# A 32-column product ahead of every second up-projection chunk

## The chip, the cores and the metric

The kernel runs on one core of a Trainium2 chip. The metric is the device time of one execution in microseconds (us). Three runs of the kernel before gave 2378.91, 2389.10 and 2390.35 us; their median is 2389.1 us. A further execution was profiled, and all rows below are of that one.

## The reference

Two transformer stacks of two layers run one after the other on 256 tokens with a model width of 1024, in float32. The first one (convolution, neighbourhood and window attention) is not touched by the change. The second one has, in each of its two layers, a feed-forward part, a mix of three attentions, and a feed-forward part again:

```python
def _swiglu(x, w1, w2):
    gt, up = jnp.split(x @ w1, 2, axis=-1)
    return (jax.nn.silu(gt) * up) @ w2
...
for l in range(DEPTH):                                    # DEPTH = 2
    x = _layer_norm(DN_ALPHA * x + 0.5 * _swiglu(x, ffn1_w1[l], ffn1_w2[l]), ...)
    mix = _token_mix(x, ...)
    x = _layer_norm(DN_ALPHA * x + mix, ...)
    x = _layer_norm(DN_ALPHA * x + 0.5 * _swiglu(x, ffn2_w1[l], ffn2_w2[l]), ...)
```

The hidden width is 2816, so `w1` is 1024 x 5632 and `w2` is 2816 x 1024. There are four such feed-forward parts.

## The kernel before

**Layout.** Activations lie transposed in SBUF, with the features on the 128 partitions and the 256 tokens along the free axis: `x[:, k, 0:256]`, `k` from 0 to 7. Weights come from one long stream in DRAM in chunks of 128 x 2048 floats (16 tiles of 128 x 128, 1 MB). A ring of four buffers in SBUF receives them; SyncE issues the DMAs (L210).

**Three products for one.** Each float32 operand is split into a high and a low part of the type `fp32r`: ScalarE rounds a chunk from `ring` to `w_hi` (L226), VectorE subtracts and writes `w_lo` (L240), both in two halves. `w_hi` and `w_lo` have two buffers each, for the even and the odd chunk. `three` (L280 to 284) then multiplies `w_hi` by the high part of the activations, `w_hi` by the low part, and `w_lo` by the high part, into one place of PSUM. Each call of `pe.matmul` becomes a weight load (PEld, 128 x 128) and a product (PE, 256 columns).

**A feed-forward stage** (`ffn_stage`) has 22 up-projection chunks and 11 down-projection chunks, and there are four stages: `ffn_stage` is called twice in each of two layers. An up-projection chunk holds the 8 tiles of the gate and the 8 tiles of the up half for 128 hidden units, so it takes 16 x 3 = 48 products; `pe_columns` writes the gate part to the first 256 columns of its place in PSUM and the up part to the next 256. ScalarE applies SiLU to the gate part (`gate`, L1895), VectorE multiplies (`hid`, L1915), GpSimd splits the result into `h_hi` and `h_lo` (L1946, L1948). A down-projection chunk takes 48 products too (L1871 to L1874, the last chunk through L282 to L284), into eight places of PSUM that stay there over the whole stage.

**Order.** Chunks come in pairs (i, s): `i` counts pairs, and s = 0 or 1 is the chunk in the pair. The first pair (the first two in the first stage) is written out, the others are the body of a hardware loop, with the same instructions and SBUF and PSUM addresses in every turn. In a stage that follows a layer norm the first chunk goes through `pe_side_by_side`. PSUM places alternate with the chunk. TensorE waits in `pe_acc` until the place was read, and in `pe_half` until a half of the chunk was split; both come ahead of the first product of the chunk, `pe_half` again ahead of the ninth tile.

**Where else short products stand in the trace.** In the attention of the second stack, products of 16 columns (L767) and transposes of 128 columns (L796) stand between the full products of L282 to L284. The prediction uses those.

Of the kernel before, what the change touches and what calls it, by code (L numbers as in the profile page):

```python
# [26 lines left out]
P = 128  # L27
D = 1024
KT = D // P
S = 256  # L30
# [85 lines left out]
def build(nc, wstream, xT, ctxT, cT, consts, vecs, rpb, rel, out):  # L116
    ctx = ExitStack()
    with ctx:
        names = {}

        def sb(name, shape, dt=F32, stack=ctx, side="left"):
            names[name] = names.get(name, 0) + 1
            if names[name] > 1:
                name = f"{name}_{names[name]}"
            return stack.enter_context(nc.sbuf_tensor(name, shape, dt, side=side))

        def count(name):
            return Count(ctx.enter_context(nc.semaphore(name)))
# [3 lines left out]
        w_hi = sb("w_hi", [P, 2, CB * P], F32R)  # L132
# [50 lines left out]
        half_read = count("half_read")  # L183
# [81 lines left out]
        def acc(s, n, at=0):  # L265

            a = 2048 * ((g0[0] + s) % 2) + at
            return psum[:, a:a + n]

        def pe_half(pe, i, s, half):  # L270

            pe.wait_ge(split_done.sem, 2 * (g0[0] + s) + 1 + half + 4 * i)

        def pe_acc(pe, i, s):

            c = g0[0] + s
            if c > 1 or not isinstance(i, int) or i:
                pe.wait_ge(acc_free.sem, c - 1 + 2 * i)

        def three(pe, o, w_cols, c, hi, lo, first, last):  # L280

            pe.matmul(o, w_hi[:, c, w_cols], hi, start=first, stop=False)  # L282
            pe.matmul(o, w_hi[:, c, w_cols], lo, start=False, stop=False)  # L283
            return pe.matmul(o, w_lo[:, c, w_cols], hi, start=False, stop=last)  # L284

        def pe_columns(pe, i, s, hi, lo, tok, kt=KT, before=None, out=None, half_read=None):

            if out is None:
                pe_acc(pe, i, s)
                out = acc(s, CB // kt * tok)  # L290
            c = (g0[0] + s) % 2
            for m in range(CB // kt):
                for k in range(kt):
                    n = m * kt + k
                    if n % (CB // 2) == 0:
                        pe_half(pe, i, s, 2 * n // CB)
                    if before and m == 0:
                        before(k)
                    mm = three(pe, out[:, m * tok:m * tok + tok], slice(n * P, n * P + P), c, hi(k), lo(k), k == 0,
                               k == kt - 1)  # L300
                    if half_read and n == CB // 2 - 1:
                        mm.then_inc(half_read.sem, 1)
            mm.then_inc(chunk_done.sem, 1)

        def pe_side_by_side(pe, hi, lo, before, tok=S):

            pe_acc(pe, 0, 0)
            pe_half(pe, 0, 0, 1)
            for k in range(KT):
                before(k)  # L310
                for m in range(2):
                    mm = three(pe, acc(0, tok, m * 512), slice((m * KT + k) * P, (m * KT + k + 1) * P), g0[0] % 2,
                               hi(k), lo(k), k == 0, k == KT - 1)
            mm.then_inc(chunk_done.sem, 1)
# [43 lines left out]
        def keep_awake(pe, n, at):  # L358

            for _ in range(n):
                pe.matmul(psum[:, at:at + P], const("ident"), const("ones_model"), start=True, stop=True)
# [1431 lines left out]
        def ffn_stage(layer, norm, more=True, bias=None):  # L1795
# [10 lines left out]
            with ExitStack() as st:  # L1806
# [5 lines left out]
                def first(i, s):  # L1812
                    return isinstance(i, int) and (i, s) == (0, 0)

                def pairs_of(eng, chunk, between=None):

                    for i in range(lead):
                        chunk(i, 0)
                        chunk(i, 1)
                        if between:  # L1820
                            between(eng, i)
                    with eng.Fori(lead, up // 2) as i:
                        chunk(i, 0)
                        chunk(i, 1)

                with nc.Block() as block:
                    @block.sync
                    def _(sp):
                        if bias:
                            bias.sync(sp)  # L1830
                        each_chunk(sp, min(up + down, CHUNKS - RING - g0[0]), lambda i, s: load_one(sp, i, s))

                    @block.tensor
                    def _(pe):
                        hi, lo = (lambda k: x_hi[:, k, at:at + S]), (lambda k: x_lo[:, k, at:at + S])
                        if norm:
                            keep_awake(pe, 6, 1536)

                        def up_chunk(i, s):
                            if norm and first(i, s):  # L1840
                                pe_side_by_side(pe, hi, lo, lambda k: norm.before(pe, k))
                            else:
                                pe_columns(pe, i, s, hi, lo, S)
                        pairs_of(pe, up_chunk, bias and bias.pe)

                        def last_chunk(i, s):

                            c = (g0[0] + s) % 2
                            pe_half(pe, up // 2 + i, s, 1)
                            pe.wait_ge(lower.sem, l0 + 2 * s + 2 + 4 * i)  # L1850
                            for m in order:
                                o = psum[:, 512 * m:512 * m + S]
                                for k in range(2):
                                    kt = 4 * i + 2 * s + k
                                    b = (k * KT + m) * P
                                    mm = three(pe, o, slice(b, b + P), c, h_hi[:, kt, :], h_lo[:, kt, :], False, k == 1)
                                mm.then_inc((chunk_done if m == order[-1] else tile_done).sem, 1)

                        def chunk(i, s, start):

                            c = (g0[0] + s) % 2
                            for k in range(2):
                                pe_half(pe, up // 2 + i, s, k)
                                kt = 4 * i + 2 * s + k
                                pe.wait_ge(lower.sem, l0 + 2 * s + k + 1 + 4 * i)
                                for m in order:
                                    if start and k == 0 and m == order[-2]:
                                        pe.wait_ge(acc_free.sem, g0[0] + up)
                                    b = (k * KT + m) * P
                                    o = psum[:, 512 * m:512 * m + S]  # L1870
                                    pe.matmul(o, w_hi[:, c, b:b + P], h_hi[:, kt, :], start=start and k == 0,  # L1871
                                              stop=False)
                                    pe.matmul(o, w_hi[:, c, b:b + P], h_lo[:, kt, :], start=False, stop=False)  # L1873
                                    mm = pe.matmul(o, w_lo[:, c, b:b + P], h_hi[:, kt, :], start=False, stop=False)  # L1874
                            mm.then_inc(chunk_done.sem, 1)
                        pe.wait_ge(acc_free.sem, g0[0] + up - 1)
                        chunk(0, 0, True)
                        chunk(0, 1, False)
                        with pe.Fori(1, down // 2) as i:
                            chunk(i, 0, False)  # L1880
                            chunk(i, 1, False)
                        last_chunk(down // 2, 0)
                        moments.pe(pe, (acc_free.sem, g0[0] + up + down))
# [1145 lines left out]
```

## Time and profile before

| | |
|---|---|
| median of three runs | 2389.1 us (2378.91 to 2390.35) |
| profiled execution, its own time | 2399.49 us |
| its span, first to last instruction | 2397.7 us |
| mean granted TensorE clock | 0.995 |
| TensorE busy, products / weight loads | 2310.4 / 2080.9 us |
| VectorE / ScalarE / GpSimd busy | 1498.1 / 1190.8 / 244.1 us |
| up-projection of stage 1, 2, 3, 4: first to last `gate` | 1025 to 1151, 1524 to 1641, 1721 to 1838, 2211 to 2323 us |

A product is shown on PE with its start and a modelled length, which is longer than the distance to the next start, since products are pipelined; the pace of the stream is the distance between starts, or the number of products in a window. Matmuls of other tiles can stand between two rows of one line. The windows view counts an instruction in each window that it touches.

### The profile page before, as it was taken

The page shows a single profiled execution, that of the slowest core. Times are in us where ns is not written, and L with a number is a line of the kernel's source. Part 1 is how long each engine was busy: PE and PEld are TensorE (multiplying, and loading weights), DVE is VectorE, ACT ScalarE, POOL GpSimd, SP SyncE. Part 2 cuts the span into 40 slices and gives each one's busy share as a digit, 9 for nine tenths or more (in the row PEclk, how much of TensorE's full clock was granted, in tenths as well). Part 3 has the DMA queues.
Part 4 walks back from the last instruction along what each step waited for, and adds up shares of the span by engine and source line. Part 5 has one row for each costly group of instructions (what it writes and reads, how often), then busy time and mean ns, then how long its engine had stood idle before and what let it go on. Part 6 is the DMA issues. An engine that isn't in the chain of part 4 may idle for free. (4 is left out here: it accounts for less than half of the span.)

```text
span 2397.7 us, 45036 instructions
## 1 busy us (share of the span) xinstructions
PE 2310.4 (96%) x17296; PEld 2080.9 (87%) x17296; DVE 1498.1 (62%) x2663; ACT 1190.8 (50%) x1934; POOL 244.1 (10%) x272
## 2 busy tenths in 40 slices
PE   6999999999989999999999899999999998999998
PEld 4777677778878689999988899999999988999998
DVE  5487874453568875655476766655655578567654
ACT  6244743543345556434366555533534466555443
POOL 0012000000012000023010100121122001000320
PEclk9999999999999999999999999999999999999999
DMA  7321023444233035455554335455455454344552
GB/s 288 120 75 58 2 106 141 160 156 158 88 121 115 19 137 180 176 197 189 192 168 156 134 133 193 153 182 193 151 182 193 149 199 136 135 165 147 205 193 88
DMA packets 61844, 355.61 MB, mean 148 GB/s; under 512 B 6208, under 2 KB 19712, under 8 KB 20352
## 3 DMA queue, kind: packets, MB, share of 16 engines
q1 hardware_dynamic: 61552, 353.55, 41.0%
q8 instruction: 102, 1.67, 0.3%
q14 instruction: 46, 0.38, 0.1%
q10 hardware_dynamic: 144, 0.01, 0.0%
HBM read 349.29 MB, written 1.10 MB: 146 GB/s over the span
## 5 line engine op out<-in xcount | busy, mean ns | idle before, releaser
L240 DVE TENSOR_TENSOR w_lo<-ring,w_hi 128x1024 fp32r<-128x1024 f32 x638 | 811.9, 1305 | 454.7 <-ACT w_hi L226 454.3
L282 PE MATMUL psum<-x_hi,w_hi 128*128 128x256 f32 (+1 forms) x3376 | 1028.3, 305 | 13.2 <-DVE x_lo L579 3.6
L283 PE MATMUL psum<-x_lo,w_hi 128*128 128x256 f32 (+1 forms) x3376 | 1009.0, 299 | 0.0
L284 PE MATMUL psum<-x_hi,w_lo 128*128 128x256 f32 (+1 forms) x3376 | 1008.7, 299 | 0.0
L226 ACT ACTIVATE w_hi<-ring 128x1024 fp32r<-128x1024 f32 (+1 forms) x638 | 643.9, 1049 | 312.0 <-PE psum L284 145.5
L282 PEld LDWEIGHTS psum<-x_hi,w_hi 128*128 128x128 f32 x3376 | 638.1, 189 | 51.9 <-issue 12.0
L283 PEld LDWEIGHTS psum<-x_lo,w_hi 128*128 128x128 f32 x3376 | 636.7, 189 | 27.2 <-issue 1.7
L284 PEld LDWEIGHTS psum<-x_hi,w_lo 128*128 128x128 f32 x3376 | 635.3, 188 | 26.3
L1871 PE MATMUL psum<-h_hi,w_hi 128*128 (+1 forms) x640 | 179.0, 280 | 0.0
L1873 PE MATMUL psum<-h_lo,w_hi 128*128 (+1 forms) x640 | 179.0, 280 | 0.0
L1874 PE MATMUL psum<-h_hi,w_lo 128*128 (+1 forms) x640 | 179.0, 280 | 0.0
L1895 ACT ACTIVATE gate<-psum 128x256 f32<-128x256 f32 x88 | 33.7, 383 | 271.7 <-PE psum L284 271.6
L881 ACT ACTIVATE probT<-psum 128x512 f32<-128x512 f32 (+3 forms) x128 | 79.5, 621 | 151.5 <-PE psum L796 151.5
L1946 POOL CAST h_hi<-hid 128x256 f32 (+1 forms) x88 | 34.9, 397 | 1014.8 <-DVE hid L1915 1014.8
L896 ACT ACTIVATE prob<-prob,neg 128x256 f32<-128x256 f32 (+6 forms) x256 | 127.6, 502 | 19.3 <-DVE neg L849 18.3
L1915 DVE SCALAR_TENSOR_TENSOR hid<-psum,gate 128x256 f32<-128x256 f32 x88 | 37.3, 424 | 138.5 <-ACT gate L1895 138.3
L1871 PEld LDWEIGHTS psum<-h_hi,w_hi 128*128 128x128 f32 x640 | 121.5, 190 | 0.0
L1873 PEld LDWEIGHTS psum<-h_lo,w_hi 128*128 128x128 f32 x640 | 120.8, 189 | 0.0
L1874 PEld LDWEIGHTS psum<-h_hi,w_lo 128*128 128x128 f32 x640 | 120.1, 188 | 0.0
L1948 POOL TENSOR_TENSOR h_lo<-hid,h_hi 128x256 f32 (+1 forms) x88 | 110.6, 1256 | 13.5 <-POOL h_hi L1946 12.7
L1494 DVE SCALAR_TENSOR_TENSOR conv_out<-cpad,vec,conv_out 128x512 f32<-128x512 f32 (+1 forms) x180 | 107.6, 662 | 0.0
L796 PEld LDWEIGHTS psum<-cst,prob 128*128 128x128 f32 (+1 forms) x544 | 58.4, 140 | 48.5 <-DVE prob L856 37.7
(332 smaller groups left out, 2859.1 us busy)
## 6 DMA issues: line engine op xcount, KB each, us to landing
ring<-wstream SPq DMA_DIRECT2D x320, 1024.0 KB, 4.8
x<-xT SPq DMA_DIRECT2D x2, 1024.0 KB, 7.7
x<-ctxT SPq DMA_DIRECT2D x2, 1024.0 KB, 10.2
rel_bias<-bias_by_distance SPq DMA_DIRECT2D x2, 1024.0 KB, 7.6
fox_bias<-forgetting_sums SPq DMA_DIRECT2D x2, 1024.0 KB, 7.5
cst<-consts SPq DMA_DIRECT2D x1, 1534.0 KB, 11.7
wk<-wk_once SPq DMA_DIRECT2D x8, 128.0 KB, 4.3
kk_sw<-kk_sw SPq DMA_DIRECT2D x8, 128.0 KB, 5.8
```

The costliest lines, as they stand in the source:

```text
L226: act.activation(w_hi[:, c % 2, h], ring[:, (c + 2 * i) % RING, h], ACT.Copy).then_inc(hi_done.sem, 1)
L240: dve.tensor_tensor(w_lo[:, c % 2, h], ring[:, (c + 2 * i) % RING, h], w_hi[:, c % 2, h].bitcast(F32), ALU.subtract).then_inc(split_done.s ...
L282: pe.matmul(o, w_hi[:, c, w_cols], hi, start=first, stop=False)
L283: pe.matmul(o, w_hi[:, c, w_cols], lo, start=False, stop=False)
L284: return pe.matmul(o, w_lo[:, c, w_cols], hi, start=False, stop=last)
L881: act.activation(self.probT[0:w, v % self.TURNS, :, 0:n], psum[0:w, at:at + wide].rearrange("p (h k) -> p h k", h=2)[:, :, 0:n], ACT.Copy) ...
L896: o = act.activation(p, p, ACT.Exp, bias=self.neg[:, t % 3, half:half + 1], accum_out=self.den[:, t % 3, half:half + 1])
L1494: dve.scalar_tensor_tensor(out=o, in0=src, scalar=wc, in1=o, op0=ALU.mult, op1=ALU.add).then_inc(conv_step.sem, 1)
L1871: pe.matmul(o, w_hi[:, c, b:b + P], h_hi[:, kt, :], start=start and k == 0, stop=False)
L1873: pe.matmul(o, w_hi[:, c, b:b + P], h_lo[:, kt, :], start=False, stop=False)
L1874: mm = pe.matmul(o, w_lo[:, c, b:b + P], h_hi[:, kt, :], start=False, stop=False)
L1948: pool.tensor_tensor(h_lo[:, j, :], hid[:, s, :], h_hi[:, j, :].bitcast(F32), ALU.subtract).then_inc(lower.sem, 1)
```

## The change

`pe_columns` gets an argument `narrow`. If it is not 0, then ahead of the first product of the chunk one product is issued with the same weight tile (`w_hi[:, c, 0:128]`) and the first `narrow` columns of the same activations, with start and stop set, into the first `narrow` columns of the same place of PSUM. The first full product follows with start set and overwrites it. In `ffn_stage` the value is `32 * s`: 0 in the first chunk of a pair, 32 in the second. No other call passes the argument.

```diff
-        def pe_columns(pe, i, s, hi, lo, tok, kt=KT, before=None, out=None, half_read=None):
+        def pe_columns(pe, i, s, hi, lo, tok, kt=KT, before=None, out=None, half_read=None, narrow=0):
...
                     if before and m == 0:
                         before(k)
+                    if narrow and n == 0:
+                        pe.matmul(out[:, 0:narrow], w_hi[:, c, 0:P], hi(0)[:, 0:narrow], start=True, stop=True)
                     mm = three(pe, out[:, m * tok:m * tok + tok], slice(n * P, n * P + P), c, hi(k), lo(k), k == 0,
                                k == kt - 1)
...
-                                pe_columns(pe, i, s, hi, lo, S)
+                                pe_columns(pe, i, s, hi, lo, S, narrow=32 * s)
```

## Rows read from the trace of the kernel before

**Rows 1.** The page: span, and busy us, share and instructions by engine.

```profile
span 2397.7 us, 45036 instructions
...
PE 2310.4 (96%) x17296; PEld 2080.9 (87%) x17296; DVE 1498.1 (62%) x2663; ACT 1190.8 (50%) x1934; POOL 244.1 (10%) x272
```

**Rows 2.** The windows view of the feed-forward stages: busy us (instructions), clock, DMA.

```profile
core 0: us, PE busy (x) PEld busy (x) DVE busy (x) ACT busy (x) POOL busy (x), PEclk, DMA share, GB/s
1055.00:1155.00 100.00, 100.00 (x852) 100.00 (x851) 58.34 (x54) 42.28 (x54) 29.41 (x36) 1.00 0.52 188
1157.00:1207.00 50.00, 50.00 (x427) 50.00 (x426) 21.25 (x18) 17.98 (x18) 0.00 (x0) 1.00 0.53 190
1530.00:1640.00 110.00, 110.00 (x936) 110.00 (x935) 64.82 (x59) 44.85 (x58) 31.75 (x39) 1.00 0.54 191
...
1727.00:1837.00 110.00, 110.00 (x936) 110.00 (x936) 64.76 (x59) 44.40 (x58) 32.44 (x39) 1.00 0.52 190
...
2220.00:2320.00 100.00, 100.00 (x885) 100.00 (x884) 60.45 (x56) 43.88 (x56) 30.50 (x38) 1.00 0.54 195
2330.00:2380.00 50.00, 50.00 (x444) 50.00 (x443) 22.56 (x23) 17.82 (x18) 0.00 (x0) 1.00 0.33 122
```

**Rows 3.** Timeline (start us, length us) of ScalarE: `gate` two chunks apart, stages 2, 4.

```profile
1601.43 0.38 ACT L1895 ACTIVATE gate<-psum 128x256 f32<-128x256 f32 x1 [3.19 <-PE psum L284]
...
1612.74 0.38 ACT L1895 ACTIVATE gate<-psum 128x256 f32<-128x256 f32 x1 [3.19 <-PE psum L284]
...
2273.92 0.38 ACT L1895 ACTIVATE gate<-psum 128x256 f32<-128x256 f32 x1 [2.97 <-PE psum L284]
...
2284.80 0.38 ACT L1895 ACTIVATE gate<-psum 128x256 f32<-128x256 f32 x1 [2.97 <-PE psum L284]
```

**Rows 4.** The timeline of PE: four 16-column products, then full ones.

```profile
1278.70 0.59 PE L767 MATMUL psum<-kkc,qa 128*128 128x16 f32 x4
1279.15 0.36 PE L282 MATMUL psum<-x_hi,w_hi 128*128 128x256 f32 x1
1279.35 0.28 PE L283 MATMUL psum<-x_lo,w_hi 128*128 128x256 f32 x1
1279.46 0.28 PE L284 MATMUL psum<-x_hi,w_lo 128*128 128x256 f32 x1
1279.58 0.28 PE L282 MATMUL psum<-x_hi,w_hi 128*128 128x256 f32 x1
```

**Rows 5.** The timeline of PE: full products, four of 16 columns, full products.

```profile
1315.27 0.28 PE L284 MATMUL psum<-x_hi,w_lo 128*128 128x256 f32 x1
1315.38 0.51 PE L767 MATMUL psum<-kkc,qa 128*128 128x16 f32 x4
1315.75 0.36 PE L282 MATMUL psum<-x_hi,w_hi 128*128 128x256 f32 x1
1315.95 0.28 PE L283 MATMUL psum<-x_lo,w_hi 128*128 128x256 f32 x1
1316.07 0.28 PE L284 MATMUL psum<-x_hi,w_lo 128*128 128x256 f32 x1
1316.18 0.28 PE L282 MATMUL psum<-x_hi,w_hi 128*128 128x256 f32 x1
1316.30 0.28 PE L283 MATMUL psum<-x_lo,w_hi 128*128 128x256 f32 x1
```

**Rows 6.** The timeline of PE: first and last restart after 16-column products.

```profile
1272.07 0.36 PE L282 MATMUL psum<-x_hi,w_hi 128*128 128x256 f32 x1
...
2011.20 0.39 PE L282 MATMUL psum<-x_hi,w_hi 128*128 128x256 f32 x1 [0.29 <-DVE qc L2199]
```

**Rows 7.** The timeline of PE: first and last restart after the transposes of L796.

```profile
1280.74 0.36 PE L282 MATMUL psum<-x_hi,w_hi 128*128 128x256 f32 x1
...
2134.79 0.36 PE L282 MATMUL psum<-x_hi,w_hi 128*128 128x256 f32 x1
```

## The prediction

> **What bounds the kernel now.** I read the page first. TensorE is the engine to look at: it is busy 96% of the span, its weight loads 87%, VectorE 62% [rows 1]. Then the windows view of the four feed-forward stages, which hold everything that the diff touches. In each stretch of them PE and PEld are busy for the whole window at a granted clock of 1.00, VectorE for about 59%, ScalarE for about 43%, and the DMA share is near 0.53 [rows 2]. So nobody feeds TensorE late there; a product added to its stream is added to the span, unless it fits into time that the stream loses anyway.
>
> The same rows show what makes this change hard to judge. In equal windows TensorE gets through different numbers of the same product: 852 in 100 us in the first stage and 885 in the last; in the down-projections 427 against 444 in 50 us [rows 2]. The timeline gives the pace. Two up-projection chunks are 2 x 48 = 96 products; from one `gate` to the next but one passes 1612.74 - 1601.43 = 11.31 us in the second stage, and 2284.80 - 2273.92 = 10.88 us in the fourth [rows 3]. That is 117.8 ns and 113.3 ns a product, at the same granted clock, with the same tiles. I call these the slow and the fast pace. In this execution stages 1, 2 and 3 ran slow from end to end (936 products in 110 us in stages 2 and 3), stage 4 fast [rows 2]. A pace, once taken, held for hundreds of products, over chunk borders too. A stage has 22 x 48 = 1056 up-products and 11 x 48 = 528 down-products; at 4.45 ns each the slow pace costs 4.7 us and 2.35 us, 7.05 us a stage, 21.1 us for the three slow stages.
>
> This also fits the spread of the times. The profiled execution took 2399.5 us (its span 2397.7 and 1.8 around it), 0.4% above the median of 2389.1. With all four stages fast it would have taken 2399.5 - 21.1 = 2378.4 us, and the fastest of the three runs took 2378.9. I infer, without seeing their traces, that runs differ by which stages run slow, and that the median run has about 1.5 of them slow. 0.5% (12 us) is about what a measurement of this kernel can tell from no change.
>
> **The change part by part.** Nothing is removed or moved. Each of the 4 stages has 11 chunks with s = 1, so 44 narrow products are added, each with a weight load of its own (in [rows 4, 5] every product has one, and L282 and L283 load the same tile of `w_hi` twice). The waits of the chunk stay ahead of the first product, the narrow one, with nothing new queued behind them; no other engine gets an instruction.
>
> *Cost of a narrow product.* No 32-column product is in the trace, but products of 16 columns are: four at L767, each with a load of 128x128. In [rows 5] the last full product before them starts at 1315.27, the first narrow one at 1315.38, the first full one after them at 1315.75 and the second at 1315.95. From 1315.27 to 1315.95 is 0.68 us; without the four it would be two steps of 0.113, 0.227 us. The four cost 0.453, or 0.113 us each. [Rows 4] show the same step: 1278.70 to 1279.15 is 0.45 for four. So the price is that of the weight load and hardly depends on the columns. It also shows the shape to expect: the full product starts early after the narrow one, and its successor late (0.20 us instead of 0.113). For one narrow product I expect some 0.113 + 0.03 + 0.20 = 0.343 us where three starts were 0.227 us apart, 0.116 us more; the starts after it can take 0.12 a few times before they settle, some 0.01 to 0.02 us. Bounds: above, 0.14 us (6.2 us in all), below, 0.03 us, the distance at which the first product after a short one starts (1315.38 + 3 x 0.112 to 1315.75), if only this were added: 1.3 us. I take 0.118 us, from the nearest rows: 44 x 0.118 = 5.2 us.
>
> The page "TensorE: Matmul & The Clock Gate" of the Trainium skill, in its section "Wait — 56ns, not 53.3ns?", gives a start-to-start floor of about 25 ns for a warm product of 32 columns; with that alone the 44 would be an estimated 1.1 us. Its section "LDWEIGHTS (loading the stationary operand)" puts a load at columns / 1.2, an estimated 107 ns for 128, and 4.7 us for 44. The 0.113 us of [rows 5] side with the load.
>
> *What it does to the pace.* This is the larger term, and its sign is open. A short product sets the stream up anew: the next two starts fall at 0.03 and 0.20 us, and then a pace is taken. In [rows 4] it is the fast one (0.11 between starts after 1279.35). In [rows 5] the stream was fast before (1315.38 - 1315.27 = 0.11), and slow after (0.12, 0.11, 0.12; nine products at the slow mean). I read all restarts of this kind in the timeline. After the 16-column products there are 14 (first and last at 1272.07 and 2011.20 [rows 6]), of which 8 end fast and 6 slow. After the 128-column products of L796 there are 54 (first and last [rows 7]), 34 fast and 20 slow. Of these 54, where the stream was fast before, 23 ended fast and 10 slow; where it was slow, 11 fast and 10 slow. So a restart takes the fast pace in about 6 of 10 cases and hangs only weakly on the pace before. Inside a loop, each pair of chunks repeats the same instructions at the same addresses, so I expect the same outcome again and again in a stage: not a mean, but one of the cases below.
>
> **The rivals.**
>
> *A. The restart ends fast, whatever came before (forecast, 0.42).* The three slow stages become fast from their first pairs on, the down-projection keeps the last pace: 2399.5 - 21.1 + 5.2 = 2383.6 us. With a few products to settle, and part of the first pairs, about 2385. For it: the majority of restarts. Against a clear win: the median run of before already has only about 10.7 us of slow pace to give back, and 5.2 are paid.
>
> *B. The pace before is kept (0.22).* The restart costs, and gives nothing: 2399.5 + 5.2 = 2404.7 against the profiled execution, 2389.1 + 5.2 = 2394.3 for a median run. For it: 23 of 33 and 10 of 21 above kept their pace.
>
> *C. It alternates, slow to fast and fast to slow (0.12).* Half of the up-chunks are slow in each stage, 4 x 4.7 / 2 = 9.4 us, and about half of the down-projections, 4.7 us: 2378.4 + 9.4 + 4.7 + 5.2 = 2397.7 us.
>
> *D. The restart ends slow (the other sign, 0.18).* One mechanism: after a narrow product the first two full starts fall where the slow pace begins, as in [rows 5], and each pair renews it. Then stage 4 is slow too, and no run has a fast stage: 2378.4 + 4 x 7.05 + 5.2 = 2411.8 us, 0.95% over the median. It decides against the change from three slow stages on: 2378.4 + 3 x 7.05 + 5.2 = 2404.8 us, 0.66% over.
>
> *E. The narrow product hides beside the next load, or does not do what it says (0.06).* If it costs 0.03 us, 1.3 us in all, and the paces stay as they are by chance, 2390.4; with all stages fast, 2379.7 us.
>
> **How the numbers follow.** The likeliest is A, 2385 us, 0.2% under the median. The range is 2379 to 2405: below, E with all fast; above, B on the profiled execution, with C inside. It leaves D out, and a part of E. Faster by over 0.5% needs 2377 us, or a set of runs of before that is as slow as the profiled one (then A is 0.6% faster): a third of A, 0.14, and 0.02 of E, together 0.16. Slower by over 0.5% is above 2401: D, 0.18, and a little of B and C, 0.22. Within 0.5%: 0.62.
>
> **What would show it.** PE gets 44 more instructions than the 17296 of [rows 1], 11 to a stage, with a form of 128x32 columns. Each is started 0.11 to 0.12 us after the L284 before it, L282 some 0.03 us later, L283 0.20 us after that. If A is right, the windows of the up stretches hold about 880 products in 100 us in all four stages, and the pair takes 10.88 + 0.12 = 11.00 us; by D it takes 11.31 + 0.12 = 11.43 everywhere; by C the chunks of a pair sequence alternate, 11.0 and 11.4. Wrong would be the forecast if the stages of one execution still differ (B), if the narrow product's price is not that of a load, or if runs of before should turn out to differ for another reason than the pace, so that 2378.4 is not a floor.

## The result, and the profile after

The change makes the kernel slower: 2403.1 us median of six runs (2401.62 to 2407.26) against 2382.3 us for six runs of before (2378.23 to 2390.35), a ratio of 1.0075 with a 95% interval of 1.0053 to 1.0098 (the quotient of the two medians is 1.0087). The profiled execution took 2405.44 us, 6.0 us more than the profiled one of before, which was itself slower than all timed runs of before.

The page of the changed kernel, span and engines:

```profile
span 2403.7 us, 45124 instructions
...
PE 2317.2 (96%) x17340; PEld 2088.7 (87%) x17340; DVE 1498.2 (62%) x2663; ACT 1190.8 (50%) x1934; POOL 242.8 (10%) x272
```

And from its groups of instructions by form:

```profile
L300 PE MATMUL psum<-x_hi,w_hi 128*128 128x32 f32 x44 | 7.9, 179 | 0.0
```

The 44 products are there, 17340 against 17296 [rows 1], each with its load. Next the windows view, for the up-projections of stages 1 to 4 and the down-projection of stages 1 and 4:

```profile
1055.00:1155.00 100.00, 100.00 (x859) 100.00 (x857) 58.51 (x53) 40.62 (x52) 29.00 (x35) 1.00 0.51 184
1157.00:1207.00 50.00, 50.00 (x427) 50.00 (x426) 21.07 (x19) 17.34 (x18) 0.00 (x0) 1.00 0.55 191
1530.00:1630.00 100.00, 100.00 (x859) 100.00 (x858) 57.11 (x53) 41.49 (x54) 28.69 (x36) 1.00 0.53 189
1727.00:1827.00 100.00, 100.00 (x860) 100.00 (x859) 57.43 (x54) 41.46 (x54) 28.73 (x36) 1.00 0.53 191
2220.00:2320.00 100.00, 100.00 (x859) 100.00 (x858) 58.60 (x53) 40.89 (x53) 29.13 (x36) 1.00 0.53 187
2330.00:2380.00 50.00, 50.00 (x427) 50.00 (x426) 21.16 (x19) 18.51 (x19) 0.00 (x0) 1.00 0.36 126
```

Before, two kinds of stage stood side by side, 852 and 885 products in 100 us [rows 2]. Now all four hold 859 or 860, near the slow end, and the down-projection of stage 4 has fallen from 444 to 427. The engines that feed TensorE do the same work as before (2663 and 1934 instructions on VectorE and ScalarE, as in [rows 1]), and the clock is 1.00 in every row.

859 is not one pace. The timeline of PE in stage 2 shows two borders between pairs, eleven microseconds apart. L300 is the new product:

```profile
1554.47 0.28 PE L284 MATMUL psum<-x_hi,w_lo 128*128 128x256 f32 x1
1554.59 0.18 PE L300 MATMUL psum<-x_hi,w_hi 128*128 128x32 f32 x1
1554.62 0.36 PE L282 MATMUL psum<-x_hi,w_hi 128*128 128x256 f32 x1
1554.82 0.28 PE L283 MATMUL psum<-x_lo,w_hi 128*128 128x256 f32 x1
...
1565.38 0.28 PE L283 MATMUL psum<-x_lo,w_hi 128*128 128x256 f32 x1
1565.49 0.28 PE L284 MATMUL psum<-x_hi,w_lo 128*128 128x256 f32 x1
1565.61 0.18 PE L300 MATMUL psum<-x_hi,w_hi 128*128 128x32 f32 x1
1565.63 0.36 PE L282 MATMUL psum<-x_hi,w_hi 128*128 128x256 f32 x1
1565.83 0.28 PE L283 MATMUL psum<-x_lo,w_hi 128*128 128x256 f32 x1
1565.95 0.28 PE L284 MATMUL psum<-x_hi,w_lo 128*128 128x256 f32 x1
1566.07 0.28 PE L282 MATMUL psum<-x_hi,w_hi 128*128 128x256 f32 x1
```

At both borders the starts look alike: the short product, the full one 0.03 us later, its successor 0.20 us after that. But the first border leads from the slow pace to the fast one, and the second from fast to slow. What tells them apart is in the weight loads. These are the groups of PEld in four neighbouring pairs of the same stage, windows 1521 to 1531, 1533 to 1542, 1544.5 to 1553.5 and 1556 to 1565 us; the last numbers are the mean ns of one load:

```profile
L282 PEld LDWEIGHTS psum<-x_hi,w_hi 128*128 128x128 f32 x29 | 5.6, 192 | 0.0
L284 PEld LDWEIGHTS psum<-x_hi,w_lo 128*128 128x128 f32 x29 | 5.4, 188 | 0.0
L283 PEld LDWEIGHTS psum<-x_lo,w_hi 128*128 128x128 f32 x28 | 5.3, 188 | 0.0
...
L284 PEld LDWEIGHTS psum<-x_hi,w_lo 128*128 128x128 f32 x26 | 5.0, 192 | 0.0
L283 PEld LDWEIGHTS psum<-x_lo,w_hi 128*128 128x128 f32 x26 | 4.9, 188 | 0.0
L282 PEld LDWEIGHTS psum<-x_hi,w_hi 128*128 128x128 f32 x25 | 4.7, 188 | 0.0
...
L283 PEld LDWEIGHTS psum<-x_lo,w_hi 128*128 128x128 f32 x26 | 5.0, 192 | 0.0
L282 PEld LDWEIGHTS psum<-x_hi,w_hi 128*128 128x128 f32 x26 | 4.9, 188 | 0.0
L284 PEld LDWEIGHTS psum<-x_hi,w_lo 128*128 128x128 f32 x26 | 4.9, 188 | 0.0
...
L284 PEld LDWEIGHTS psum<-x_hi,w_lo 128*128 128x128 f32 x27 | 5.1, 188 | 0.0
L283 PEld LDWEIGHTS psum<-x_lo,w_hi 128*128 128x128 f32 x27 | 5.1, 188 | 0.0
L282 PEld LDWEIGHTS psum<-x_hi,w_hi 128*128 128x128 f32 x27 | 5.1, 188 | 0.0
```

In the slow pace one load of each three takes 192 ns and the other two 188. There are three slow paces, then, by the place of the long load: I call them slow-282, slow-284 and slow-283. In the fast pace (the fourth pair) all three take 188. Each new product moves the stream one step: slow-282, slow-284, slow-283, fast, and slow-282 again. I could read the pace before and after 41 of the 44 products. Fast went to slow-282 in 12 of 12, slow-282 to slow-284 in 11 of 11, slow-284 to slow-283 in 10 of 10, slow-283 to fast in 8 of 8. Of the 84 up-chunks behind the first one of each stage 20 ran fast, about one in four. Two of the 20 have another cause: between the first pairs of stage 1 stand 12 and then 4 products of 512 columns for the position bias (L1778), 0.43 us apart, and behind each of the two groups the stream came out fast here, though it had gone in as slow-282. The last pair left all four down-projections slow in this execution.

### The profile page after: what moved, and what is told of

Its sections match the earlier page's. It is cut to its first block and busy times, and to the rows that moved or that the text cites. A ratio compares the mean times of both kernels' runs of the same rounds, so it can differ in the third digit from the quotient of the medians.

```text
span 2403.7 us, 45124 instructions
## 1 busy us (share of the span) xinstructions
PE 2317.2 (96%) x17340; PEld 2088.7 (87%) x17340; DVE 1498.2 (62%) x2663; ACT 1190.8 (50%) x1934; POOL 242.8 (10%) x272
## 5 line engine op out<-in xcount | busy, mean ns | idle before, releaser
L282 PE MATMUL psum<-x_hi,w_hi 128*128 128x256 f32 (+1 forms) x3376 | 1033.0, 306 | 12.8 <-DVE x_lo L581 3.3
L284 PE MATMUL psum<-x_hi,w_lo 128*128 128x256 f32 (+1 forms) x3376 | 1009.9, 299 | 0.0
L282 PEld LDWEIGHTS psum<-x_hi,w_hi 128*128 128x128 f32 x3376 | 637.2, 189 | 51.4 <-issue 12.0
L284 PEld LDWEIGHTS psum<-x_hi,w_lo 128*128 128x128 f32 x3376 | 637.8, 189 | 26.2
```

## The experiments

The edits are against the changed kernel. The added products are always overwritten by the full one behind them, so no kernel leaves work out. Where one time stands, it is that of the profiled execution. Such a single time holds more than the pace. In the 14 profiles of this case the stretch ahead of the first `gate` takes from 1023.1 to 1026.8 us, though the kernels differ by at most two products there, and the one from the last `gate` of stage 3 to the first of stage 4 takes 370.8 to 373.9 us with a fast down-projection. So the pace is read from the stages themselves, and whole times are only a check to within some 3 us.

**1. The kernel before, profiled again.** No edit.

> The kernel before, profiled a second time. Theory (each feed-forward stage takes a pace at its start and keeps it, and executions differ by which stages run slow): the count of slow stages tells the time, 2378 us plus 7.05 us for each slow stage; no stage changes its pace inside. Rival (the time of an execution differs for another reason, for instance the loading of weights in the first half): the same stages as in the first profile are slow and the time still differs by several us, or the fast stages do not match the time within 3 us.

2392.72 us. The windows of the up-projections of stages 1 to 4:

```profile
1055.00:1155.00 100.00, 100.00 (x852) 100.00 (x851) 58.84 (x54) 41.61 (x53) 29.39 (x36) 1.00 0.53 187
1530.00:1630.00 100.00, 100.00 (x852) 100.00 (x850) 57.69 (x53) 41.06 (x53) 28.86 (x36) 1.00 0.53 189
1727.00:1827.00 100.00, 100.00 (x885) 100.00 (x884) 60.28 (x55) 42.20 (x55) 29.22 (x36) 1.00 0.55 198
2220.00:2320.00 100.00, 100.00 (x884) 100.00 (x884) 61.10 (x56) 42.82 (x55) 29.83 (x37) 1.00 0.54 197
```

Two stages slow this time, where three were: 2378.4 + 2 x 7.05 = 2392.5 us was due. That this meets the measured time within 0.2 us is in part luck, since the stretch ahead of the first `gate` is 0.7 us shorter than in the first profile and the attention ahead of stage 4 about 1.2 us longer. Stage 3 alone shows the price: 112.0 us from its first to its last `gate` instead of 116.5. The same kernel takes either pace in stage 3. The 23 runs of before that were timed beside experiments 7 and 8 and the twelve runs of 5 fit too: 3 lie at 2378.5 to 2379.6, 18 at 2384.2 to 2388.3, and 2 at 2390.1 and 2390.3 us, with a gap of 4.6 us between the first two groups; one slow stage is due at 2385.5. They have no traces, so that the groups are counts of slow stages is argued. Two more timed runs of before, of 2376.8 and 2382.9 us, show that 2378.4 is a floor only to within 2 us or so.

**2. A full product instead of a short one.**

```diff
-                                pe_columns(pe, i, s, hi, lo, S, narrow=32 * s)
+                                pe_columns(pe, i, s, hi, lo, S, narrow=256 * s)
```

> The extra product has all 256 columns instead of 32; it is overwritten by the next one as before. Theory T1 (it is the short product that sets up the stream anew; a full one is a product like the others): 44 x 0.113 = 5.0 us of price, and each stage keeps one pace from end to end, so 2383 us plus 7.05 us for each slow stage. Rival T2 (49 products in a chunk, that is the longer loop body or the shift against the three-product pattern, makes the slow pace): the same cycle of one fast and three slow pairs as in the changed kernel, 2403 to 2407 us. Where a stage is slow, T1 still allows the longer weight load to move by one place in the trio with each extra product.

2389.08 us. Stages 2 and 3 ran fast from end to end, stage 4 slow from end to end (windows of stages 2 and 4, the second of 90 us):

```profile
1530.00:1630.00 100.00, 100.00 (x885) 100.00 (x884) 59.33 (x55) 42.29 (x54) 29.43 (x36) 1.00 0.54 189
...
2220.00:2310.00 90.00, 90.00 (x767) 90.00 (x766) 52.06 (x47) 36.43 (x47) 25.95 (x32) 1.00 0.52 185
```

Stage 1 was slow in its first pair only; there the added product had moved slow-282 to slow-284, and it was the 12 products of L1778 behind the pair that left the stream fast. With 29 fast-to-fast borders in the loops, the number 49 does not make the slow pace, and T2 falls. In stage 4 the long load moves by one place a pair and comes round in three, as the groups of PEld in four neighbouring pairs show (windows 2191 to 2200, 2202.5 to 2211.5, 2214 to 2223, 2225 to 2234 us):

```profile
L282 PEld LDWEIGHTS psum<-x_hi,w_hi 128*128 128x128 f32 x26 | 5.0, 192 | 0.0
...
L284 PEld LDWEIGHTS psum<-x_hi,w_lo 128*128 128x128 f32 x26 | 5.0, 192 | 0.0
...
L283 PEld LDWEIGHTS psum<-x_lo,w_hi 128*128 128x128 f32 x26 | 5.0, 192 | 0.0
...
L282 PEld LDWEIGHTS psum<-x_hi,w_hi 128*128 128x128 f32 x26 | 5.0, 192 | 0.0
```

So the long load falls on every third product of the stream whatever the product is, and one product more shifts it against the lines of the code. Of the two added products tried so far only the short one enters or leaves the fast pace.

**3. Other widths: 128, 64, 16 columns.** The same line with `128 * s`, `64 * s`, `16 * s`.

> The extra product has 128 columns. Theory T1 (any product shorter than the weight load lets the next one start early and sets the stream up anew): the cycle of the changed kernel, one fast pair and then three slow ones, 2403 to 2407 us. Rival T3 (the cycle depends on how early the next product starts, so on the width): another sequence of paces, between 2383 us (all fast) and 2412 us (all slow).

> The extra product has 64 columns, shorter than the weight load like 32. Theory (what counts is only that the product ends before the next load does): the table of 32, one fast pair in four, 2403 to 2407 us. Rival (the width sets it, as 128 did): the two-step table of 128 or another, 2396 to 2399 us if half of the pairs are fast.

> The extra product has 16 columns. Both theories expect the table of 32 here, one fast pair in four and 2403 to 2407 us; another table would mean that even the shortest products differ. The price per product should stay at 0.112 us, since the weight load sets it.

2398.12, 2405.00 and 2405.05 us. Each width had its own cycle, the same in all stages. 16 columns gave that of 32, 18 of 84 chunks fast. 64 columns gave fast, slow-282, slow-283, fast, with 27 of 84 fast, so my "table of 32" for it was wrong. 128 columns alternated fast and slow-282, 41 of 84 fast. The stages follow the share of fast chunks: from first to last `gate`, the four of them add up to 476.3 us with 16 columns, 475.9 with 32, 474.5 with 64 and 471.7 with 128. That the whole times of 16 and 64 columns are equal comes from elsewhere, above all from the first `gate`, which the execution with 64 columns reached 2.4 us later. So T3 holds: the width sets the table, and not only that the product is short.

The first border of stage 4 adds a step that the cycles don't hold. With 128 columns the stream came there as slow-283, and went on fast. These are groups of PEld before and behind that product (windows 2201.3 to 2202.6 and 2204.5 to 2208 us); behind it, L284 and L282 have 188 too:

```profile
L283 PEld LDWEIGHTS psum<-x_lo,w_hi 128*128 128x128 f32 x4 | 0.8, 191 | 0.0
...
L283 PEld LDWEIGHTS psum<-x_lo,w_hi 128*128 128x128 f32 x11 | 2.1, 188 | 0.0
```

With 64 columns it came there as slow-284 and went on fast as well (L284 at 190 ns in 2205.2 to 2206.5 us, 188 in 2209 to 2212 us).

**4. The short product ahead of both chunks.**

```diff
-                                pe_columns(pe, i, s, hi, lo, S, narrow=32 * s)
+                                pe_columns(pe, i, s, hi, lo, S, narrow=32)
```

85 products come of it, since the first chunk of stages 2 to 4 goes through another function.

> The 32-column product stands ahead of both chunks of a pair, 87 or so products instead of 44. Theory T1 (each short product moves the stream one step through fast, slow with the long load at L282, at L284, at L283, and back to fast): the cycle runs per chunk and not per pair, one chunk in four fast; the price doubles to 9.8 us: 2408 to 2412 us. Rival T4 (the period of four comes from something that repeats every four pairs, such as the ring of weight buffers or the DMAs): the fast chunks still lie four pairs apart, and their share changes.

2411.25 us. The same four steps now pass in four chunks instead of four pairs, at least 19 times each, and 21 of 84 chunks are fast. T4, the ring of four buffers, is out.

**5. 192 columns.** The same line with `192 * s`.

> The extra product has 192 columns. Theory (each width has a fixed table from the pace before to the pace after; 32: fast to slow at L282, to slow at L284, to slow at L283, to fast; 128: fast to slow at L282 to fast; 256: fast stays, slow moves one place): a table of its own, the same in all four stages and in every pair. If the stream is mended by it from every pace and stays fast, all stages run fast after their first pair, 2383 us. Rival (outcomes at random): within one stage the same pace before is followed by different ones.

2381.22 us, 22 us below the median of the changed kernel with the same number of products. All 41 borders read within the stages went fast to fast, and the first one of stage 4 went from slow-284 to fast. The timeline of PE and the windows of stages 2 and 3:

```profile
1524.33 0.28 PE L284 MATMUL psum<-x_hi,w_lo 128*128 128x256 f32 x1
1524.45 0.25 PE L300 MATMUL psum<-x_hi,w_hi 128*128 128x192 f32 x1
1524.53 0.30 PE L282 MATMUL psum<-x_hi,w_hi 128*128 128x256 f32 x1
1524.67 0.28 PE L283 MATMUL psum<-x_lo,w_hi 128*128 128x256 f32 x1
```

```profile
1530.00:1630.00 100.00, 100.00 (x885) 100.00 (x884) 59.41 (x55) 43.03 (x56) 29.42 (x36) 1.00 0.53 189
1727.00:1820.00 93.00, 93.00 (x823) 93.00 (x822) 55.99 (x51) 39.60 (x51) 28.09 (x34) 1.00 0.53 192
```

The next start comes after 0.08 and 0.14 us here, not after 0.03 and 0.20. Twelve timed runs:

> The 192-column product ahead of every second chunk again, now in rounds. Theory (a product of 192 columns keeps the fast pace and leads a slow one back to it): every run has all stages fast, so the times lie within about 3 us of each other at 2378 + 44 x 0.113 = 2383 us, a ratio to before of 0.998 to 1.002, since runs of before have between none and three slow stages. Rival (the all-fast stages of the single look were luck of their entries): the times spread over 2383 to 2404 us as those of before do.

2383.9 us (2382.12 to 2385.70, 12 runs) against 2386.2 us of before (23 runs), a ratio of 0.9992 (0.9983 to 1.0000): no clear difference. The spread is 3.6 us, against 11.9 for before. Its profile shows all stages fast but for the first pair of stage 1, behind which again the products of L1778 stand, and the first chunk of stage 4, which came as slow-284 and was mended by the first product of 192 columns. The 44 products eat what they mend.

**6. Two short ones in a row.** A product of 256 columns and one of 128 ahead of each second chunk:

```diff
-                    if narrow and n == 0:
-                        pe.matmul(out[:, 0:narrow], w_hi[:, c, 0:P], hi(0)[:, 0:narrow], start=True, stop=True)
+                    if narrow and n == 0:
+                        for width in narrow:
+                            pe.matmul(out[:, 0:width], w_hi[:, c, 0:P], hi(0)[:, 0:width], start=True, stop=True)
...
-                                pe_columns(pe, i, s, hi, lo, S, narrow=32 * s)
+                                pe_columns(pe, i, s, hi, lo, S, narrow=(256, 128) if s else ())
```

> Two extra products ahead of every second chunk, one of 256 columns and one of 128. By the tables of the earlier runs: from fast, 256 keeps it and 128 makes it slow at L282; from slow at L282, 256 moves it to L284, and 128 then meets a pace that no run has shown it. If 128 turns L284 into fast, the stage alternates; if it turns it into slow at L282, the pair repeats slow, all slow: 2378 + 28 + 10 = 2416 us. This run reads the missing places of the table. The price is 88 x 0.112 = 9.9 us.

2410.70 us, in a cycle of fast, slow-282, slow-283, fast, which neither of my two branches had. By the table of 256 the pair's 128 met slow-284 on the second step and made it slow-283, and met slow-282 on the third and made it fast. The pace between the two products can't be read, so the step of 128 from slow-284 is inferred.

**7. From which slow paces 192 columns lead out.** The product may now also stand ahead of the up half (`n == 8`), where an accumulation starts too:

```diff
-                    if narrow and n == 0:
-                        pe.matmul(out[:, 0:narrow], w_hi[:, c, 0:P], hi(0)[:, 0:narrow], start=True, stop=True)
+                    if narrow and k == 0 and (n == 0 or twice):
+                        pe.matmul(out[:, m * tok:m * tok + narrow], w_hi[:, c, n * P:n * P + P], hi(0)[:, 0:narrow], start=True, stop=True)
...
-                                pe_columns(pe, i, s, hi, lo, S, narrow=32 * s)
+                                pe_columns(pe, i, s, hi, lo, S, narrow=192 if s else 32)
```

and in the second kernel with `twice=not s`.

> 32 columns ahead of the first chunk of a pair, 192 ahead of the second. By the tables so far 32 makes a fast stream slow at L282. Theory (192 leads slow at L282 straight back to fast): the chunks of each pair alternate, slow at L282 and fast, in all stages; up-projections half slow, down-projections fast: 2378 + 9.4 + 87 x 0.113 = 2397 us. Rival (192 moves slow paces on like 256 does, and only some of them become fast): a longer cycle, and 2400 us or more.

> 32 columns ahead of both halves of the first chunk of a pair, 192 ahead of the second chunk. From fast, 32 and 32 again give slow at L284 by the table of 32. Theory (192 leads every slow pace to fast): the first chunk is slow, its first half at L282 and its second at L284, the second chunk is fast, pair after pair: 2378 + 9.4 + 129 x 0.113 = 2402 us. Rival (192 has a table in which slow at L284 is not followed by fast): another pace in the second chunk, and a cycle over several pairs.

2401.92 and 2401.71 us. The first followed the rival: 192 moved slow-282 on to slow-284 (19 times) and led slow-283 to fast (19 times), so the fast chunk comes once in four, and 2378.4 + 14.1 + 85 x 0.113 = 2402.1 us would be due. I had expected slow-282 to be mended. The second followed the theory. Its groups of PEld in the two halves of a first chunk and in the next chunk (windows 1526.3 to 1528.4, 1529.2 to 1531.4, 1533 to 1537 us) hold these lines, for the last window all three:

```profile
L282 PEld LDWEIGHTS psum<-x_hi,w_hi 128*128 128x128 f32 x6 | 1.2, 192 | 0.0
...
L284 PEld LDWEIGHTS psum<-x_hi,w_lo 128*128 128x128 f32 x7 | 1.3, 192 | 0.0
...
L282 PEld LDWEIGHTS psum<-x_hi,w_hi 128*128 128x128 f32 x13 | 2.4, 188 | 0.0
L283 PEld LDWEIGHTS psum<-x_lo,w_hi 128*128 128x128 f32 x12 | 2.3, 188 | 0.0
L284 PEld LDWEIGHTS psum<-x_hi,w_lo 128*128 128x128 f32 x12 | 2.3, 188 | 0.0
```

That is slow-282, slow-284, and after the 192 fast. These are the steps as read, for an added product that stands between full ones of 256 columns. None had an exception; those marked "once" were read a single time:

| from | 32 (and 16) | 64 | 128 | 192 | 256 |
|---|---|---|---|---|---|
| fast | slow-282 | slow-282 | slow-282 | fast | fast |
| slow-282 | slow-284 | slow-283 | fast | slow-284 | slow-284 |
| slow-284 | slow-283 | fast (once) | slow-283 (inferred) | fast | slow-283 |
| slow-283 | fast | fast | fast (once) | fast | slow-282 |

Only the column of 192 keeps the fast pace and leads all slow ones to it, in at most two products. In experiments 4 and 7 the 32-column product also stands right behind the products of L1778 and at the start of stage 1; there is no pace ahead of it there, and the table says nothing of such places.

**8. A version that beats both.** With the `pe_columns` of experiment 7, two products of 192 columns in each written-out first pair of a stage (stage 1 has two such pairs), and none in the loop; 10 in all.

```diff
-                                pe_columns(pe, i, s, hi, lo, S, narrow=32 * s)
+                                pe_columns(pe, i, s, hi, lo, S, narrow=192 if s and isinstance(i, int) else 0, twice=True)
```

> Products of 192 columns only in the written-out first pairs (one pair; two in the first stage), in the chunk with s = 1, ahead of its gate half and ahead of its up half: 10 in all instead of 44, 1.1 us. Theory (once a stage is fast it stays fast): 2378 + 1 = 2380 us with hardly any spread, 0.1 to 0.3% under the median of before. If two mending products are too few for some slow pace, single runs lie 7 us higher, and the profile shows that stage slow from end to end.

2380.0 us (2377.80 to 2383.71, 12 runs) against 2386.2 us (23 runs), a ratio of 0.9978 with an interval of 0.9969 to 0.9988, and 1.0% below the changed kernel by the medians. Small, but clear of 1; against the 2382.3 us that before had in the first comparison it would be 0.1%. The spread of 5.9 us is half that of before, not the "hardly any" that I expected. The profiled execution, at 2383.71 us the slowest of the twelve, shows that the pace of the four stages can't be all of this spread: they ran fast, but its first `gate` came 2.2 us later than in experiment 5, and the stretch from the last `gate` of stage 3 to the first of stage 4 took 373.9 us instead of 371.0. The windows of the up-projections of stages 1 and 4, 90 us each:

```profile
1055.00:1145.00 90.00, 90.00 (x796) 90.00 (x795) 54.68 (x51) 39.55 (x51) 28.28 (x34) 1.00 0.55 197
...
2220.00:2310.00 90.00, 90.00 (x796) 90.00 (x796) 54.06 (x50) 39.81 (x51) 27.13 (x34) 1.00 0.54 195
```

Stage 1 came in as slow-282 here, and its first two products of 192 columns made it fast. Stage 4 came in as slow-284, and the first one did. Stages 2 and 3 came in fast by themselves.

## Why the prediction was wrong, by its own steps

**The number.** The forecast was 2385 us, 0.2% below before; the change came out slower. That 2403.1 us lies inside the range of 2379 to 2405 is luck: the upper end is case B on the profiled execution, 2404.7 us with three stages slow and one fast, and nothing of that kind happened.

**Right: what bounds the stages, and the two paces.** TensorE was the bound, a pace was kept over a stage of before, and its price of 7.05 us a stage held within what experiment 1 can tell. The stretches of the changed kernel add up in the same way. From the first to the last `gate`, stage 4 went from 112.0 to 116.9 us, and from there to the end of the span from 74.9 to 77.2; stages 1 to 3, slow before, went from 125.6, 116.5 and 116.5 to 125.6, 116.9 and 116.5. Four to six fast chunks in each of them (0.21 us apiece) nearly paid for the 11 more products. With 1.5 us less ahead of the first stage, that is the 6.0 us between the two profiled executions.

**Right: the price of a product.** I took 0.118 us. A chunk of 49 products in a slow pace that stayed slow took 5.765 us against 5.653 for 48, which is 0.112; within the fast pace (experiment 5) 5.553 against 5.440, 0.113. Starts at 0.03 and 0.20 us came as forecast, though the merged row of four in [rows 5] could not tell which start is the early one: there the 0.03 us lie between the first and the second short product, and the other starts are 0.11 us apart. By the section "LDWEIGHTS (loading the stationary operand)" of the page "TensorE: Matmul & The Clock Gate" of the Trainium skill the load takes an estimated 107 ns, 5% below the 0.112 us measured. The floor of about 25 ns a start in its section "Wait — 56ns, not 53.3ns?" agrees with the first start (0.03 us); the next start, at 0.20 us, pays it back.

**Wrong: the step from the restarts to a chance, and with it the term of 21.1 us.** Case A took the slow pace of three stages away, 21.1 us. In the profile the slow chunks and down-projections came to about 14.1 + 9.4 = 23.5 us, so that the paces cost 2.4 us instead of giving back 21.1; the price of the products, 4.9 us, was near the 5.2 forecast. The step that failed is how A got its chance. The tally of 68 restarts in the attention said that 6 of 10 end fast, and that the pace before matters little (23 of 33 stayed fast). In this stream the pace before decides everything: from fast, the 32-column product ended slow 12 times of 12. The tally mixed streams of one to four short products of several widths, after products of other types and with waits between, and it put three slow paces into one row. The nearest cases lay in the trace of before: of the 14 restarts after 16-column products only four came straight out of full products, the two from fast ended slow (1315.38 and 2001.85 us), and of the two from slow one ended slow and one fast. [Rows 5] is one of the two from fast, and I weighed it as one of 14. They are four short products in a row, and four steps of the table's first column would lead from fast back to fast, so the table doesn't carry over to them either.

**Wrong: "the same outcome again and again in a stage".** This is what took the repeat of one case for granted. The same instruction at the same address has an outcome that depends on where the long load stands, and that moves. None of the cases A to E describes a four-step cycle. D had the mechanism for the step from fast; C had the alternation, with two steps instead of four, and the number of fast chunks wrong (half, not a quarter).

**What the time should have been.** From all stages fast: 44 x 0.112 = 4.9, three quarters of the up-chunks slow 14.1, the down-projections slow 4 x 2.35 = 9.4: 2406.8 us, where the profile has 2405.4 and the median 2403.1. The median lies low by 3.7 us, and two causes are open, since the timed runs have no trace. A stage that enters the cycle one step later can end fast, and saves 2.35. Or it has nothing to do with the paces: the profiled executions of the two kernels that were timed twelve times (experiments 5 and 8) were also the slowest of their twelve, by 1.8 and 3.7 us over the median, with their stages fast.

**Baseline.** I counted on 1.5 slow stages in a median run of before; its new median of 2382.3 means, by the same sum, about half a stage. Against the old median of 2389.1 the loss would have been 0.6%; against the new one it is 0.9% by the medians and 0.75% by the ratio of the runs.

**Open.** What makes a stage of before come in fast or slow; where the differences of 3 us ahead of the first `gate` and in the attention come from; why the third load takes 4 ns longer and why that costs the trio 13 ns in all, and what in a width makes its column of the table. Nothing here separates an access of SBUF from a rhythm inside TensorE.

## What to carry to other kernels

If a stream of equal products shows two paces at the same clock, find what tells them apart in the loads before you weigh an intervention, and read its effect as a table from state to state, not as a rate. A disturbance that only moves the stream from one state to the next, as the 16- and 32-column products did, gives each state its share and nothing more; look for one with a fixed point at the good state, and apply it once, where the state is set. Before comparing two versions within 1%, profile the old one twice, since a single profile can have three slow stages where, by its time, the median has about one or less. And go by the stretches that the change touches: here the rest of the execution varied by 3 us on its own.

## What the runs showed of the hardware that was not expected

- Products of 256 columns with a weight load each run at 113.3 ns or at 117.8 ns a start, at a granted clock of 1.00, with the same operands, and hold that for over 1000 products. The slow pace has a load of 192 ns on every third product and 188 on the others.
- Between full products, an added product of 16 to 128 columns always threw the stream out of the fast pace; one of 192 or 256 columns never did.
- Groups of 12 and 4 products of 512 columns changed the pace as well: in the changed kernel slow-282 went in and fast came out of both; in experiment 2, and in the profile of the twelve runs of 5, slow-284 went into the first and fast came out; in both profiles of before slow-283 went in and slow-283 came out.
- The steps between the paces were the same in all executions and stages that met them, the 19 and more of each kind in experiment 4 included.
